# Splitting h by block instead of by half, at a multiple of 512 bytes, with the constant tables made on the chip

## The reference

```python
def swiglu(h, w_in, w_out):
    gate, up = jnp.split(h @ w_in, 2, axis=-1)
    return (jax.nn.silu(gate) * up) @ w_out

def second_block(x, ...):
    for i in range(DEPTH_2):
        x = x + 0.5 * rms_norm_2(swiglu(rms_norm_2(x, g[0]), ff1_w_in[i], ff1_w_out[i]), g[1])
        h = rms_norm_2(x, g[2])
        m = mixer_a(...)  # or mixer_b, mixer_c, by layer
        x = x + rms_norm_2(m, g[3])
        x = x + 0.5 * rms_norm_2(swiglu(rms_norm_2(x, g[4]), ff2_w_in[i], ff2_w_out[i]), g[5])
```

## Time and profile before

| | |
|---|---|
| median of 3 runs | 2545.04 us |
| the profiled execution | 2543.71 us |
| its span in the trace | 2541.9 us |
| TensorE matmul busy | 2526.3 us, 99%, 15929 instructions |
| VectorE busy | 1771.3 us, 70% |
| ScalarE busy | 1398.6 us, 55% |
| mean DMA rate | 181 GB/s |
| granted TensorE clock | 0.999 of full |

### The profile page before, as it was taken

One profiled execution on the slowest core, in us unless ns is written; L12 is line 12 of the kernel. 1 busy time (PEld: TensorE's weight loads), 2 busy tenths in 40 slices (PEclk: granted clock), 3 DMA queues, 4 the chain that ended last, 5 costly groups with the idle time before them and its releaser, 6 DMA issues.

```text
span 2541.9 us, 38596 instructions
## 1 busy us (share of the span) xinstructions
PE 2526.3 (99%) x15929; PEld 2258.0 (89%) x15929; DVE 1771.3 (70%) x2517; ACT 1398.6 (55%) x2098; POOL 156.4 (6%) x228
## 2 busy tenths in 40 slices
PE   9999999999999999999999999999999999999998
PEld 8999898998988988888888888888988888898887
DVE  7778567785775777757657775775777577566773
ACT  7766476663554565545555554554655455455552
POOL 2100011000000000000010000002010000010000
PEclk9999999999999999999999999999999999999999
DMA  7267552665665556556564665655456566563763
GB/s 236 92 178 210 172 166 84 183 195 169 207 193 198 182 162 195 188 186 198 185 220 147 203 194 185 193 191 194 152 166 199 188 181 202 188 204 123 216 189 126
DMA packets 568442, 459.96 MB, mean 181 GB/s; under 512 B 10315, under 2 KB 529435, under 8 KB 568267
## 3 DMA queue, kind: packets, MB, share of 16 engines
q1 hardware_dynamic: 562759, 441.91, 55.2%
q0 software_dynamic: 4656, 15.30, 1.7%
q10 hardware_dynamic: 851, 0.28, 0.0%
HBM read 456.37 MB, written 1.10 MB: 180 GB/s over the span
## 4 chain that ended last, share of the span: by engine, by line
PE 94%; DVE 3%; ACT 1%; DMA 1%; issue 0%; POOL 0%; DVEq 0%; POOLq 0%; ACTq 0%
PE ps L917 27%; PE ps L800 23%; PE ps L799 11%; PE ps L782 5%; PE ps L783 5%; PE ps L784 5%; PE ps L735 4%; PE ps L736 4%; PE ps L737 4%; PE ps L802 1%; PE ps L658 1%; DVE wlo L1891 1%; PE ps L1018 1%; PE ps L1004 0%; DVE xc L2550 0%; DMA raw<-in_w_in 0%
## 5 line engine op out<-in xcount | busy, mean ns | idle before, releaser
L1891 DVE TENSOR_TENSOR wlo<-raw,whi 128x2048 fp32r<-128x2048 f32 (+1 forms) x419 | 956.8, 2287 | 362.8 <-ACT whi L1315 362.6
L1315 ACT ACTIVATE whi<-raw 128x2048 fp32r<-128x2048 f32 (+2 forms) x421 | 800.3, 1906 | 306.3 <-DMA raw<-in_ff_w_out 161.6
L800 PE MATMUL ps<-h,whi 128*128 128x512 f32 x2560 | 873.7, 393 | 0.0
L799 PE MATMUL ps<-h,wlo 128*128 128x256 f32 x2240 | 629.7, 281 | 0.0
L800 PEld LDWEIGHTS ps<-h,whi 128*128 128x128 f32 x2560 | 459.7, 188 | 81.2
L799 PEld LDWEIGHTS ps<-h,wlo 128*128 128x128 f32 x2240 | 421.9, 188 | 15.3
L1315 ACT ACTIVATE u<-ps 128x512 f32<-128x512 f32 x160 | 96.0, 600 | 398.9 <-PE ps L800 398.9
L917 PE MATMUL ps<-whi,hid_hi 128*128 128x512 f32 x880 | 291.3, 390 | 0.0
L917 PE MATMUL ps<-whi,hid_lo 128*128 128x512 f32 x880 | 290.5, 389 | 0.0
L917 PE MATMUL ps<-wlo,hid_hi 128*128 128x512 f32 x880 | 290.4, 389 | 0.0
L782 PE MATMUL ps<-h,whi 128*128 128x256 f32 x1024 | 288.0, 281 | 0.0
(11 more groups left out here) (322 smaller groups left out, 3196.4 us busy)
## 6 DMA issues: line engine op xcount, KB each, us to landing
raw<-in_ff_w_in SPq DMA_DIRECT2D x176, 1024.0 KB, 5.6
raw<-in_ff_w_out SPq DMA_DIRECT2D x88, 1024.0 KB, 4.9
raw<-in_ffn_w_in SPq DMA_DIRECT2D x44, 1024.0 KB, 5.7
raw<-in_a_w_qkv SPq DMA_DIRECT2D x24, 1024.0 KB, 5.0
raw<-in_ffn_w_out SPq DMA_DIRECT2D x22, 1024.0 KB, 4.9
raw<-in_w_in SPq DMA_DIRECT2D x18, 1024.0 KB, 6.0
raw<-in_c_w_qkv SPq DMA_DIRECT2D x12, 1024.0 KB, 5.0
raw<-in_w_out SPq DMA_DIRECT2D x8, 1024.0 KB, 4.9
```

The costliest lines, as they stand in the source:

```text
L799: e.matmul(out[:, 0:SEQ], lo, m.h[:, 0, k, :], start=False, stop=False, skip_group_check=True)
L800: ins = e.matmul(view(out, a=2), hi, m.h[:, :, k, :], start=(k == 0), stop=(k == KT - 1), skip_group_check=True)
L1315: return self.nc.scalar.activation(*a, **k)
L1891: self.e.tensor_tensor(chunk_view(m.wlo[:, slot, :], c), chunk_view(m.raw[:, slot, :], c), chunk_view(m.whi[:, slot, :], c).bitcast(F32), ...
```

## The change

The layout of `h` becomes [128, 8, 2, 256]: the high and the low half of block k stand next to each other, so that the 512 columns of a wide product are one run. The two spacers go, so `h` begins at 116736, a multiple of 512, and everything behind it moves down by 512 bytes and keeps its place relative to 512. Five tables are no longer loaded: three are set by memset at the start and the others are worked out on VectorE from the ones that are still loaded. In the scaled edges ScalarE writes `h_hi` of the first tile before a sum of squares, VectorE writes `h_lo` of the first tile before a residual add, and in all edges that use `rstd_halves` GpSimd adds EPS to the first half's sum while it waits for the second.

```diff
@@ constants(), CONST
-    add("ones", np.ones((P, P)))
-    add("zeros", np.zeros((P, P)))
-    add("causal", np.where(c <= r, 0, BIG))
-    add("upto_add", np.where(r <= c, 0, BIG))
     add("from_neg", -(r >= c).astype(np.float32))
-    add("ones_neg", -np.ones((P, P)))
-    add("strict_add", np.where(r < c, 0, BIG))
+MADE = CONST["dist"][0]
+for _n in ("ones", "zeros", "causal", "upto_add", "ones_neg"):
+    CONST[_n] = (MADE, MADE + P)
+    MADE += P
@@ Tensor.wide_chunk
-                    e.matmul(out[:, 0:SEQ], lo, m.h[:, 0, k, :], start=False, stop=False, skip_group_check=True)
-                ins = e.matmul(view(out, a=2), hi, m.h[:, :, k, :], start=(k == 0), stop=(k == KT - 1), skip_group_check=True)
+                    e.matmul(out[:, 0:SEQ], lo, m.h[:, k, 0, :], start=False, stop=False, skip_group_check=True)
+                ins = e.matmul(out, hi, m.h[:, k, :, :].rearrange("p a b -> p (a b)"), start=(k == 0), stop=(k == KT - 1), skip_group_check=True)
@@ Scalar.edge, scaled
             self.split(1, 0)
+            self.turn_hi(0, gain)
             self.square_new(1, 0)
-            self.turn_hi(0, gain)
             self.square_new(1, 1)
@@ Vector.start
+        for name, value in (("ones", 1.0), ("zeros", 0.0), ("ones_neg", -1.0)):
+            e.memset(m.cst(name), value)
@@ Vector.edge
-            self.add_sum(1, 0)
+                self.add_sum(1, 0)
             self.turn_lo(0, gain)
+            if scaled:
+                self.add_sum(1, 0)
             self.add_sum(1, 1)
@@ Vector.mix, first layer
-            e.wait_ge(s.tables_in, 32)
-            for i, mask in enumerate((m.ident, m.strict)):
-                ins = e.tensor_copy(m.masks[:, i, :], mask)
-            ins.then_inc(s.masks_made, 1)
+            e.wait_ge(s.tables_in, 16)
+            e.tensor_copy(m.masks[:, 0, :], m.ident)
+            e.tensor_scalar(m.masks[:, 1, :], m.cst("from_neg"), -BIG, None, ALU.mult)
+            e.tensor_scalar(m.cst("causal"), m.cst("from_neg"), 1.0, BIG, ALU.add, ALU.mult)
+            e.tensor_scalar(m.cst("upto_add"), m.upto, -1.0, -BIG, ALU.add, ALU.mult).then_inc(s.masks_made, 1)
+            e.wait_ge(s.masks_made, 1)
@@ Pool.rstd_halves
+        e.wait_ge(s.m_squares, self.sums + 2 * t + 1)
+        self.link(e.tensor_scalar(ms[:, t:t + 1], m.ss2[:, t, 0:1], EPS, None, ALU.add))
         e.wait_ge(s.m_squares, self.sums + 2 * t + 2)
-        self.link(e.tensor_tensor(ms[:, t:t + 1], m.ss2[:, t, 0:1], m.ss2[:, t, 1:2], ALU.add))
-        self.link(e.tensor_scalar(ms[:, t:t + 1], ms[:, t:t + 1], EPS, None, ALU.add))
+        self.link(e.tensor_tensor(ms[:, t:t + 1], ms[:, t:t + 1], m.ss2[:, t, 1:2], ALU.add))
@@ build
-        sb(ctx, "in_front_of_h", [P, 8])
-        m.h = sb(ctx, "h", [P, 2, KT, SEQ], F32R)
-        sb(ctx, "behind_h", [P, 120])
-        m.h_hi, m.h_lo = m.h[:, 0, :, :], m.h[:, 1, :, :]
+        m.h = sb(ctx, "h", [P, KT, 2, SEQ], F32R)
+        m.h_hi, m.h_lo = m.h[:, :, 0, :], m.h[:, :, 1, :]
```

More of the change, by code:

```diff
@@ L548, in mix @@
             if l == 0 and b == 4:
-                e.dma_start(m.consts[:, CONST["upto"][0]:], d.consts[:, CONST["upto"][0]:CONST["dist"][0]]).then_inc(s.tables_in, 16)
-                e.dma_start(m.strict, d.consts[:, CONST["strict_add"][0]:CONST["strict_add"][1]]).then_inc(s.tables_in, 16)
+                e.dma_start(m.consts[:, CONST["upto"][0]:CONST["dist"][0]], d.consts[:, CONST["upto"][0]:CONST["dist"][0]]).then_inc(s.tables_in, 16)
         self.advance(IN_CHUNKS)
@@ L3048, in build @@
             [("b_w", [P, 8, P]), ("b_rows", [P, 2, D]), ("b_uv", [P, TT, 2 * D]), ("b_wt", [P, 8, P])])
-        m.consts = sb(ctx, "consts", [P, CONST["dist"][0]])
+        m.consts = sb(ctx, "consts", [P, MADE])
         m.cols = sb(ctx, "cols", [P, ROW_TILES * P])
@@ L3108, in build @@
         m.ext = z1[0:32, 576:576 + 3 * P]
-        m.strict = m.z2[:, 0, 0:P]
         m.y = m.xc[:, 0:2, :]
```

## The result

The changed kernel takes 2552.14 us, the median of 9 runs (2551.59 to 2552.95), against 2545.04 us for the kernel before (9 runs, 2543.79 to 2547.09). The ratio is 1.0028, with a 95% interval of 1.0020 to 1.0037: slower by 7.1 us, more than the 0.2% that can be told. The forecast was a gain of 2.5 us.

A forecast was written before the change was run, and what follows sets the result against it. TensorE, busy 2526.3 of 2541.9 us, was taken as the bound. Place of h -1.0, edges -1.0 and root -0.3 gave -2.3 us: 2541.4 on the profiled execution, forecast as 2542.5 in terms of the median, range 2510 to 2557.

The forecast's parts named there:

- x: Start-to-start distance of a 256-column TensorE product with both operands at 0; taken as 119 ns, each ns worth 8.4 us.
- the wide term: Wide stages, 2560 pairs of a 512- and a 256-column product: from 348.8 ns to 226.7 + x, -7.9 us.
- A fixed sum per product, both sides aligned: TensorE products with both operands at 0: extra beyond columns nearly fixed, 13.4 ns for 512 columns, about 12.3 for 256.
- rivals 1 and 2: 256-column products stay near 116.7 ns, 2523 us, chance 0.24; or extra is a share of columns, 113.3 ns, 2495, chance 0.14.
- Feature chunks, +7.1 us: 3072 products of 256 columns with h moving: from 116.7 ns to x, 119, a loss of 7.1 us.
- Token tiles, +3.3 us: 2784 products of 256 columns with h stationary: from 117.8 ns to x, 119, a loss of 3.3 us.
- Out products, -3.5 us: 528 products of 512 columns with h stationary: from 233.3 to 226.7 ns, a gain of 3.5 us.
- Scaled edges, -1.0 us: Two scaled edges: TensorE's idle 0.36 us and short refill, about 0.5 us each, go; -1.0 us, bounds 0 and -1.7.
- Root, -0.3 us: GpSimd's rstd_halves: one step of 0.29 us leaves the chain, gaining 0.3 us at the kernel's end only, nothing between stages.
- Tables, 0: Start of the kernel: masks cost VectorE about 0.6 us, covered by its 1.60 us idle; net 0, bounds -0.5 and +0.6.
- rival 3: Feature chunks and token tiles lose at 120 ns, wide pair stays at 348.8: +11.4 us, 2556, chance 0.14.
- Rival 4: Alignment of h does nothing, only edges and tail remain: -1.3 us, 2544, chance 0.10.

The follow-up runs named there:

- the map: Changed kernel with extra rows of 32 products and of 16 wide pairs behind its last product, h at sixteen places; 256 columns took 113.3 to 120.0 ns, total time not comparable.
- The third kernel: Changed kernel with the old layout of h and its start at 32 put back, new tables, edges and root kept: 2540.36 us, ratio 0.9982.

## Why the prediction was wrong

The step that failed is the size of x, "I take 119", and a second one is the wide term, which counted on the settled pair for every half. The sum was zero at x = 119.1, each ns of x was worth 8.4 us, and x is 120.0 in settled stretches of the feature chunks and in the map. The earlier trace rows had both numbers: 118 for six distances and 120 for the last three. I averaged over a row that had not settled, where the last ones were the better reading. This 1 ns is 8.4 us, enough by itself to turn the forecast gain into a loss. The pattern behind the turn cost 6.3 us more in the wide pairs (+0.9 measured against the -5.4 that x = 120 gives). And the claim that two rows of one class fix the sum for a difference of 8 us was too bold at 8.4 us to the ns.

Point by point:

- *A fixed sum per product, both sides aligned.* The form held: 226.7 for 512 and 120.0 for 256 columns are 13.4 and 13.3 ns over the columns. It holds in the map at 0 and 256 and not in general: at 64 it has 113.3 and 233.3. And "Rows 5 to 9 agree that it is fixed rather than a share" was a misreading: rows 5 and 8, with `h` at 32, are 10.0 and 20.0 ns over the columns, which is a share of them. So the rule by which I left rivals 1 and 2 out is no law of the engine, but a row of a map. The Trainium skill (TensorE: Matmul & The Clock Gate, Back-to-back issue gap) has 2.5 ns beside the columns, and calls that the gap of an isolated product; for a stream it has about 131 ns at 512 columns. Neither is met here: the least lasting extra at 256 columns is 113.3 - 106.7 = 6.6 ns, and 512 columns never take less than 226.7 ns as a settled mean of equal products.
- *Wide, -7.9 us.* Measured +0.9, the second miss. The pair was expected at 226.7 + 119 = 345.7 ns and came at 349.8; at x = 120 the same term would have been 2560 x (346.7 - 348.8) = -5.4 us. The settled pair was right (347 ns in the second half); what I did not see is that the turn at k = 0 can carry a dearer pattern through a whole half, and does in 153 of 312. The earlier trace rows hinted at it: eight pairs at 348.8 with three at 346.7. I had put the rest down to the turn itself.
- *Feature chunks, +7.1 us.* Measured +9.4; by x = 120 it would be +10.1.
- *Token tiles, +3.3 us.* Measured +5.0; by 120, +6.1.
- *Out products, -3.5 us.* Measured -3.7, which is right by luck. The settled 226.7 is as forecast, but between the two kernels that differ in the place alone the term is -2.3 us, as faster products also come sooner to waits that stay. The other 1.4 are mostly the waits at the two scaled edges, which the new order takes away and which stand behind an out product.
- *One run instead of two, nothing.* Right: old and new layout at 32 differ by 0.4 us.
- *Scaled edges, -1.0 us.* The idle time is gone as described. The medians of the edit alone give 0.1 with an interval of 2.3 us either way; its trace has 1.5 us, half as much again as forecast and inside the bounds. The wait ahead of tile 1, which I had left in place, shrinks as well, from 0.27 to 0.12 us between starts.
- *Root, -0.3 us.* The saved step was sized right, 0.28 us, and its reach was not: I wrote that TensorE "waits for nothing of this size" at the edges. The view of L1998 would have shown otherwise: TensorE's transposes wait for it in five places, and at eleven edges they lose 0.12 us without any idle time. Measured -3.4 us (0.9979 to 0.9996, so -1.0 to -5.3).
- *Tables, 0.* The third kernel has tables, edges and root at -4.2 us; root and edges apart gave -3.4 and -0.1. The rest of 0.7 us is far inside the intervals. The tables alone were not run.

At x = 120, with the wide term of -5.4, the prediction's own sum would have been -5.4 + 10.1 + 6.1 - 3.5 = +7.3 for the place, and with the -1.3 of the edges and the end 2543.7 + 6.0 = 2549.7 on the profiled execution, 2551.0 in terms of the medians. With the wide gain gone it is rival 3, 2556. The measurement lies between. Rival 3's picture of what happens came true (feature chunks at 120, wide pair at its old average), and of the 3.9 us by which its time is too high, 2.9 are the larger gain of the smaller edits (4.2 for 1.3). Its mechanism, two streams that meet at each start, is not shown: at 96 the feature chunks are as dear as at 0. Its chance of 0.14 was too low for a case that needed only 0.9 ns more on a number with two readings. Rival 4 is refuted: the Trainium skill (SBUF: State Buffer, the cachelines note) has lines of 16 bytes, so 16, 48, 64 and 96 would all be alike, and here they lie between 2537.2 and 2555.1.

Why a pair of places costs what it costs stays open. The map is one execution, and it shows what happens and not by which part.

## What to carry to other kernels

In a kernel like this one, with TensorE full and products of 256 or 512 columns, the place of the moving operand against the stationary one is worth up to 6 or 7 ns on each product, and neither "aligned" nor "shifted" is good in itself. Measure settled rows of the kernel's own products, in their own order, at several places, and add them up by the kernel's counts before moving anything. And before an edit off the critical engine is costed at nothing, ask the view of the line that it feeds who waits for that line. When two traces are compared, take the distance from a point behind the start, which here differed by a microsecond or two between executions.

## What the runs showed of the hardware

- The distance of equal products settles into a pattern that depends on the place, and the mean is set by it: 113.3 to 120.0 ns for 256 columns, 226.7 to 234.2 for 512. Moving both operands by the same multiple of 32 bytes leaves 256 columns at 119.9 to 120.0; moving `h` alone by 32 takes them to 116.7 where it moves and to 118.3 where it is stationary.
- There are several lasting patterns at one place. At 64 the stretches of feature chunks run at 113.3 or at 117.8 ns. In the changed kernel a wide half runs at 352 or at 347 ns per pair (for the first, (701.54 - 698.72) / 8 = 352.5).
- The same turn in the order of two products at k = 0 costs 5.5 us at 0 and saves 9.9 us at 64.
